# Prompt attention: probabilities left in the scores' PSUM banks, and the causal mask of the row-maximum blocks added by VectorE

## The reference, cut to what is computed

```
logits = einsum('bqhd,bkhd->bhqk', qblk, k) * scale
logits = logits + cblk[..., None] - ck_t[:, :, None, :]
mask   = k_pos[None, :] <= pblk[:, None]
logits = where(mask, logits, -inf)
probs  = softmax(logits, axis=-1)
out    = einsum('bhqk,bkhd->bqhd', probs, v)
```

## Time and profile before

| what | value |
|---|---|
| median of 3 runs | 1980.89 us (1978.67 to 1981.26) |
| the profiled execution's own time | 1982.06 us |
| its span, first to last instruction | 1980.2 us |
| busy TensorE matmul, VectorE, ScalarE, GpSimd | 1894.0 (96%), 1310.9 (66%), 846.6 (43%), 230.0 (12%) us |
| head 0, 1102.5 to 1161.1: TensorE, VectorE, ScalarE busy | 58.60, 46.12, 37.49 of 58.60 us |
| head 4, 1331.5 to 1387.9: the same | 54.67, 50.91, 39.40 of 56.40 us |
| head 7, 1501.7 to 1546.4: the same | 42.74, 35.51, 37.45 of 44.70 us |

### The profile page before, as it was taken

The page is one execution under the profiler, slowest core; times in us unless marked ns, Lnnn a source line. Parts: engine busy times, 40 slices in busy tenths (PEclk is TensorE's granted clock), DMA queues, the critical chain, the costliest instruction groups (busy, mean ns, idle before and its releaser), DMA issues. The chain is left out here.

```text
span 1980.2 us, 28779 instructions
## 1 busy us (share of the span) xinstructions
PE 1894.0 (96%) x10726; PEld 1732.3 (87%) x10726; DVE 1310.9 (66%) x2127; ACT 846.6 (43%) x1529; POOL 230.0 (12%) x165
## 2 busy tenths in 40 slices
PE   4999999999999999999999999999999899999998
PEld 3899999999999999999999777777777699998886
DVE  7788888955455465444655688889987544455654
ACT  4454555534343442433323576666678710111100
POOL 4000000000000000000000202333323520000111
PEclk9999999999999999999999899999999999999999
DMA  5599898969888886879897715566554598665441
GB/s 182 199 305 321 286 309 306 299 233 303 290 290 296 288 299 193 300 238 312 264 295 249 159 42 105 120 129 126 121 102 137 168 340 277 212 209 153 138 142 68
DMA packets 272750, 435.99 MB, mean 220 GB/s; under 512 B 63236, under 2 KB 139156, under 8 KB 268476
## 3 DMA queue, kind: packets, MB, share of 16 engines
q1 hardware_dynamic: 272612, 434.16, 70.0%
HBM read 285.18 MB, written 148.78 MB: 219 GB/s over the span
## 5 line engine op out<-in xcount | busy, mean ns | idle before, releaser
L751 ACT ACTIVATE fr_wq<-fr_raw 128x512 fp32r<-128x512 f32 x288 | 178.0, 625 | 200.8 <-PE fr_d L617 137.0
L1665 DVE TENSOR_TENSOR at_p_lo<-at_p,at_p_hi 128x512 fp32r<-128x512 f32 (+1 forms) x320 | 228.0, 721 | 42.3 <-ACT at_p_hi L1635 41.7
L1634 ACT ACTIVATE at_p<-at_s 128x512 f32<-128x512 f32 (+1 forms) x320 | 170.6, 533 | 116.1 <-PE at_s L1558 68.1
L615 PE MATMUL fr_b<-fr_xh,fr_wq 128*128 128x348 f32 x576 | 189.0, 328 | 14.0 <-DVE fr_u L1120 10.5
L1009 DVE TENSOR_TENSOR fr_wq<-fr_raw,fr_wq 128x512 fp32r<-128x512 f32 x288 | 192.8, 684 | 8.7 <-ACT fr_wq L751 5.0
L615 PE MATMUL fr_c<-fr_xh,fr_wq 128*128 128x348 f32 x576 | 187.0, 325 | 4.4 <-DVE fr_wq L1009 2.5
L615 PE MATMUL fr_a<-fr_xh,fr_wq 128*128 128x348 f32 x576 | 187.9, 326 | 2.4 <-DVE fr_wq L1009 1.8
L616 PE MATMUL fr_a<-fr_xl,fr_wq 128*128 128x348 f32 x576 | 187.2, 325 | 0.0
L617 PE MATMUL fr_a<-fr_xh,fr_wq 128*128 128x348 f32 x576 | 186.6, 324 | 0.0
L617 PE MATMUL fr_b<-fr_xh,fr_wq 128*128 128x348 f32 x576 | 186.3, 323 | 0.0
L616 PE MATMUL fr_b<-fr_xl,fr_wq 128*128 128x348 f32 x576 | 186.3, 323 | 0.0
(11 more groups left out here) (314 smaller groups left out, 4578.5 us busy)
## 6 DMA issues: line engine op xcount, KB each, us to landing
fr_wq<-w_mixed SPq DMA_DIRECT2D x192, 512.0 KB, 5.6
fr_raw<-w_tiles SPq DMA_DIRECT2D x96, 512.0 KB, 5.5
w_mixed<-fr_wq SPq DMA_DIRECT2D x96, 512.0 KB, 4.6
mg_gates<-merge_gates SPq DMA_DIRECT2D x40, 416.0 KB, 4.6
fr_raw<-w_tiles SPq DMA_DIRECT2D x48, 256.0 KB, 5.5
merge_gates<-fr_res SPq DMA_DIRECT2D x32, 348.0 KB, 6.7
mixed<-mg_mixed SPq DMA_DIRECT2D x40, 208.0 KB, 3.8
ln_h<-h_rows SPq DMA_DIRECT2D x16, 512.0 KB, 3.3
```

What stands on the lines that cost most here:

```text
L615: pe.matmul(to, wh[:, idx, k, :], xh[:, idx, k, :], start=first, stop=False, skip_group_check=skip)
L751: act.activation(wh[:, idx], operand(i, idx), ACT.Copy).then_inc(w_hi[idx], 1)
L1634: act.activation(p[:, r, cols], s_bank[r][:, cols], ACT.Exp, scale=SCALE)
L1665: dve.tensor_tensor(p_lo[:, r, cols], p[:, r, cols], p_hi[:, r, cols].bitcast(F32), ALU.subtract)\
```

## The change

It does two things.

First, `p` in SBUF is gone. ScalarE writes `p_hi` first, and then the float32 exponential back into the scores' own PSUM bank. `low` on VectorE reads that bank and `p_hi`. The bank is given back to TensorE by `lo_done` (VectorE's subtraction), no longer by `p_done`; the counts that were started ahead by four (`RING`) move from `p_done` to `lo_done`.

Second, the 16 small mask products of a head's max blocks are gone from TensorE. A row `wide_mask` of 512 columns in SBUF (384 zeros and then the causal triangle, which TensorE turns once at the start of the stage) is added on VectorE: `tensor_tensor_reduce` adds it to the bank, writes the sum back into the bank and gives the row's maximum. The off-diagonal units keep the plain maximum. The mask products of `scores` stay.

```diff
-        p = sb("p", [P, RING, QW], 28672)
+        wide_mask = sb("wide_mask", [P, QW], 28672)
...
-                pe.wait_ge(p_done, NS * h + st + 1)
+                pe.wait_ge(lo_done, NS * h + st + 1)
...
-                pe.wait_ge(lo_done, NS * h + st + 1)
+                pe.wait_ge(lo_done, NS * h + st + 1 + RING)
...
-                last = pe.matmul(bank[:, 0:width], qm[h % 3][0:HD + 2, i * P:(i + 1) * P], km[h % 3][0:HD + 2, c * QW:end],
-                                 start=True, stop=(c < i // 4))
-                if c == i // 4:
-                    last = pe.matmul(bank[:, width - P:width], mask_b[:, :], eye_b[:, :], start=False, stop=True)
-                last.then_inc(unit_done, 1)
+                if h == 1 and u == 1:
+                    pe.wait_ge(mask_made, 2)
+                pe.matmul(bank[:, 0:width], qm[h % 3][0:HD + 2, i * P:(i + 1) * P], km[h % 3][0:HD + 2, c * QW:end],
+                          start=True, stop=True).then_inc(unit_done, 1)
...
+            pe.matmul(m_bank[1][:, 0:P], mask_b[:, :], eye_b[:, :], start=True, stop=True).then_inc(mask_turned, 1)
             for st in range(LEAD):
                 scores(0, 0, st)
...
-                act.activation(p[:, r, cols], s_bank[r][:, cols], ACT.Exp, scale=SCALE)
-                act.activation(p_hi[:, r, cols], s_bank[r][:, cols], ACT.Exp, scale=SCALE).then_inc(p_done, 1)
+                act.activation(p_hi[:, r, cols], s_bank[r][:, cols], ACT.Exp, scale=SCALE)
+                act.activation(s_bank[r][:, cols], s_bank[r][:, cols], ACT.Exp, scale=SCALE).then_inc(p_done, 1)
...
-                dve.wait_ge(p_done, NS * h + st + 1 + RING)
-                dve.tensor_tensor(p_lo[:, r, cols], p[:, r, cols], p_hi[:, r, cols].bitcast(F32), ALU.subtract)\
+                dve.wait_ge(p_done, NS * h + st + 1)
+                dve.tensor_tensor(p_lo[:, r, cols], s_bank[r][:, cols], p_hi[:, r, cols].bitcast(F32), ALU.subtract)\
                    .then_inc(lo_done, 1)
...
-                dve.tensor_reduce(piece_max[:, i, c:c + 1], bank[:, 0:width], AX_X, ALU.max)\
-                   .then_inc(unit_read, 1)
+                if c < i // 4:
+                    dve.tensor_reduce(piece_max[:, i, c:c + 1], bank[:, 0:width], AX_X, ALU.max)\
+                       .then_inc(unit_read, 1)
+                else:
+                    dve.tensor_tensor_reduce(out=bank[:, 0:width], in0=bank[:, 0:width], in1=wide_mask[:, QW - width:QW],
+                                             scale=1.0, scalar=-3e38, op0=ALU.add, op1=ALU.max,
+                                             accum_out=piece_max[:, i, c:c + 1]).then_inc(unit_read, 1)
...
+            dve.memset(wide_mask[:, 0:QW - P], 0.0).then_inc(mask_made, 1)
+            dve.wait_ge(mask_turned, 1)
+            dve.tensor_copy(wide_mask[:, QW - P:QW], m_bank[1][:, 0:P]).then_inc(mask_made, 1)
+            dve.wait_ge(mask_made, 2)
             low(0, 0)
```

More of the change, by code:

```diff
@@ L1424, in prompt_attention @@
         unit_read = sem("unit_read")
+        mask_turned, mask_made = sem("mask_turned"), sem("mask_made")
         maxed, split, turned, rows_done = sem("maxed"), sem("split"), sem("turned"), sem("rows_done")
@@ L1453, in prompt_attention @@
         st_.rows_done = rows_done
-        st_.all_p, st_.all_pv, st_.all_read = (p_done, NS * H + RING), (pv_done, NS * H + RING), (o_read, NQ * H + 2)
+        st_.all_p, st_.all_pv, st_.all_read = (lo_done, NS * H + RING), (pv_done, NS * H + RING), (o_read, NQ * H + 2)
         st_.head6_done = pv_done, NS * (H - 1) + RING
@@ L1622, in scalar @@
         def scalar(act):
-            act.sem_inc(p_done, RING)
+            act.sem_inc(lo_done, RING)
             act.sem_inc(pv_done, RING)
```

## The result

The kernel after takes 1949.2 us (median of 6 runs, 1945.9 to 1950.27) against 1981.08 for the kernel before (6 runs): ratio 0.9845, 95% interval 0.9834 to 0.9856. Two more comparisons of the same pair gave ratios of 0.9838 (0.9825 to 0.9852) and 0.9856 (0.984 to 0.9873). One run of the kernel before, beside the first three experiments, took 2090.49 us at a granted clock of 0.85 and is left out of every comparison. The forecast was 1958 us with a range from 1944 to 1974: the direction and the main mechanism came out, and the gain is 8 us larger than forecast.

What follows compares the result with a forecast made beforehand. VectorE was taken to bound the 30 steps with max blocks, only because p_lo was stretched; otherwise TensorE would. Terms -17.4 - 3.0 - 1.8 - 1.4 = -23.6 us took 1982.06 to 1958.5, stated as 1958, range 1944 to 1974.

Steps and rivals of the forecast that it cites:

- the main mechanism: In heads 1 to 6, p_lo read from PSUM is no longer stretched beside GpSimd's SBUF products: -17.4 us.
- The stretching of `p_lo`: Heads 1 to 6: p_lo with one operand in PSUM runs undisturbed by GpSimd, 2.9 us a head, -17.4 us.
- Head 7: Last head, no max blocks, TensorE bounds: its waits for p_lo, between 2.0 and 4.0 us, go; middle taken, -3.0 us.
- The mask part in heads 1 to 6: Mask products leave TensorE, masked maxima load VectorE: 0.3 us a head gained in the 30 steps, -1.8 us.
- TensorE alone remains: Rival: masked maximum nearly free, 30 steps take 40 us, last ten go as in head 0; 1947 us, chance 0.10.
- Head 0: First head, TensorE bounds, partly at half clock: seven mask products saved there, turned mask costs 0.3; -1.4 us.
- ScalarE and the bank's release: Exponentials' order, writing the second into its own bank, and TensorE's wait for p_lo before reusing it: no added time.
- The rule that spoke against the change: VectorE's fixed cost, 120 cycles from PSUM against 58: 65 ns more per p_lo, whole kernel some 1972 us.

Runs made afterwards that it cites:

- the first three experiments: Kernel before with only p kept in the bank, only the masked maximum, or GpSimd's work on y mostly left out: 1956.08, 1975.55, 1953.91 us against 1978.59.
- the bank alone: Kernel after with TensorE's mask products and VectorE's plain maxima restored, only p staying in the scores' banks: 1956.08 us against 1978.59 for the kernel before.

## Why the prediction was right, and where its sizes were off

**The stretching of `p_lo`** (forecast -17.4 in heads 1 to 6) is the mechanism, and was sized rightly: with the bank alone these heads take 322.9 us against 340.4, -17.5. The estimate from head 0's undisturbed steps carried over without loss. The prediction took VectorE as the bound of all 30 steps; TensorE bounds the first 16 already (21.88 us with and without stretching). The term did not suffer, since it was read from steps 16 to 30.

**Head 7** (forecast -3.0): 44.61 to 40.86 us, -3.8. Of the two bounds in the earlier trace rows the weight loads' 4.0 was the truer one, not the middle.

**The mask part in heads 1 to 6** (forecast -1.8) is the term that was mis-sized: 322.9 us with the bank alone, 316.5 to 316.7 after, so -6.3, or 1.05 a head in place of 0.3. Three numbers in it were wrong.

- The masked maximum was charged 0.10 us and costs some 0.01 at most (0.60 to 0.61 us from start to start at 512 columns, like a plain one; five of them change nothing in 22.46 us of a fully busy VectorE). So VectorE's 39 us stay below TensorE's and never become the bound.
- The 30 steps without stretching were set at 41.1 us, which takes the mean's gain of 2.9 off head 4's 44.0. Head 4 had less stretching than the mean; the bank alone takes 41.36.
- The forecast then let only 0.3 us through because two engines with equal load would wait for each other. In the trace the 30 steps fall to 40.3, with TensorE busy in nearly every microsecond.

By the price in the earlier trace rows, 16 products of 0.12 us leave TensorE, an estimated 1.9 a head. About 0.9 of that does not come out, and the weight loads' waits for the max have grown by as much (7.0 + 2.2 us in heads 1 to 6, against 3.8 with the bank alone, below: 5.4 / 6). That the one is the other is argued from this agreement; no run shows it.

```profile
PEld at_m L1585 <- DVE at_piece_max L1671: 3.8, 18, 0.3
```

The fast case among the rivals, TensorE alone remains, was thus right about the 30 steps (40.3 us measured, 40 said there) and wrong about the last ten, which stayed at 12.4 for a reason that it did not name, the negated maxima beside GpSimd. The forecast's own time for the 30 steps was 40.6 to 41.1.

**Head 0** (forecast -1.4): -0.7 to -1.0 among executions with a like start, -5.4 in the two profiles first compared.

**ScalarE and the bank's release** (forecast nothing): 591 against 594 ns, and no row in which TensorE's scores wait for `p_lo`. Right.

Summed for like starts: -17.5 - 3.8 - 6.3 and about -1 for head 0 make -28.6, against the forecast's -23.6; nearly all of the difference is the mask part. The three pairs of medians differ by 31.9, 32.3 and 28.0 us. What the first two have beyond 28.6 was not taken apart: a long start at half clock is worth 4 us, but only the profiled executions are known to have had one or not, and what follows the stage took 433 to 434 us in the profiles of the kernel before and 434 to 437 in those of the kernel after, which goes the other way.

That the time fell into the range is in part owed to the range, which took in both neighbours: 1949.2 us is at the very edge of the forecast's own 1949 to 1967, and nearer to the fast rival's 1947 than to 1958.

The rule that spoke against the change, the Trainium skill's larger fixed cost for VectorE instructions that read PSUM ("VectorE: DVE Perf Modes", the section on the TRN2 errata), is not borne out here: `p_lo` of 512 columns takes 683 ns on average from PSUM and SBUF, and 683 from SBUF twice when GpSimd is quiet.

## What to carry to other kernels

Where a VectorE instruction with two SBUF operands runs beside GpSimd and its duration scatters (0.68 to 1.8 us here), move one operand into a PSUM bank that is already held. Written in place it cost neither a bank nor ScalarE time here (591 against 594 ns), and holding the bank until the subtraction cost nothing, since TensorE waited for the same subtraction anyway. Before pricing such a change, cut a loop at the points where the second engine begins and ends its work, and name the bound of each stretch: the same mask edit was worth 3.2 us in heads 1 to 6 before the stretching was gone and 6.3 after, because VectorE bounded 14 of the 30 steps as long as `p_lo` was stretched. Small instructions count too: in the trace 0.8 us a head hung on one of 128 x 16.

## What the hardware showed that was not expected

- An addition and a maximum over one PSUM and one SBUF operand run at the pace of a plain maximum: 0.60 to 0.61 us from start to start at 512 columns, 0.01 more at most. The accumulator's reading shows as a record of 140 ns that takes no time of its own.
- A one-operand instruction was held up as well: 128 x 16 from SBUF to SBUF took 0.98 us beside GpSimd and 0.17 with its input in PSUM. The Trainium skill, "SBUF — State Buffer", section "Who interferes with whom", lists that operation among those that can take the pair of ports that VectorE shares with GpSimd; the two rows of it in the experiments agree.
- The start of head 0 at half clock ended between 1107 and 1116 us in executions of one and the same kernel, which moves head 0 by 4 us.
